# The query projection of the expert layer from unsplit weights: full fp32 products, seven chunks loaded ahead, three rows of the second table fetched early

## The chip, the cores and the metric

One core of one Trainium2 chip runs the whole program in one launch. The metric is the device time of that launch in microseconds, measured several times; beside it stands one profiled execution, whose trace gives every time in this document that is not called the median. PE is TensorE, DVE VectorE, ACT ScalarE, POOL GpSimd and SP the engine whose queue issues most weight loads.

## What is computed

256 tokens of width 2048 pass through two blocks. The first has a gated recurrence, a dilated attention and a convolutional feed-forward. The second has a recurrent and a spatial gating half and then the layer that this change touches (`peer`): 8 query heads of 256 columns, each scored against two sets of 128 keys; the best 16 of each side give 256 pairs, and the best 16 pairs name 16 of 16384 experts. So each token needs 128 rows of each of two tables, `expert_u` and `expert_v`.

```python
q = (x @ w_q).reshape(B, S, PEER_HEADS, 2, PEER_HALF)
s = jnp.einsum('bshpk,hpnk->bshpn', q, sub_keys)
top_s, top_i = lax.top_k(s, PEER_TOPK)
...
u = jnp.take(expert_u, it, axis=0)
act = jax.nn.gelu(jnp.einsum('td,tkd->tk', xt, u)) * gt
v = jnp.take(expert_v, it, axis=0)
return jnp.einsum('tk,tkd->td', act, v)
```

A final norm with `final_norm_g` follows.

## The kernel before

All weights but the tables come as one stream of blocks (`stream_blocks`), each cut into chunks of 1 MB, each chunk into two halves called subs (`sub`, numbered 0 to 751; the last 32, 720 to 751, are the weight `peer_w_q`, called `wq` below: 8 blocks of 4 subs, one block per head). SP loads chunks into a ring of `NR = 3` buffers `raw`; ACT rounds a sub to the high part `wh` (float32r) and DVE takes the low part `wl = raw - wh`; PE forms every product in three float32r matmuls (high by high, high by low, low by high). These are lines L1158, L1159 and L1160 for `wq`. `u5` holds the transposed input, itself as a high and a low part. A chunk is loaded when the chunk three before it has been split (`s_lo`), and a block's result goes to one of two pairs of banks, which ACT (L1463) copies to `qTt`. PE then multiplies with the keys (`key_scores`, L1288), ACT keeps the scores (`keep_scores`, L1613), and DVE chooses: `top_sides`, `top_pairs`, `top_ids` (its last instruction, L2154, writes the row numbers `ids` of one head for 128 tokens) and `top_weights`. Before that, `turn_keys` transposes the keys `kyN`, which POOL has loaded during the projection before `wq` (`w_out_2`, blocks 116 to 119, of which the order below shows `u` as operand).

Row n of `peer_u` is then gathered for 128 tokens at once: one indirect DMA of 128 x 8 KB = 1.049 MB, issued by POOL (`get_u`, L2253) into one of `NU = 4` buffers `Ub`. It waits for its ids and for dot n - 4 to be done. DVE forms the dot products (`dot`, L2169); each fourth time ACT takes the gelu and DVE multiplies by the gates. Row n of `peer_v` goes likewise (`get_v`, L2261) into one of `NV = 11` buffers `Vb`, and PE adds it, times a diagonal matrix from ACT (`diag`), to the output banks (`spread`, L1303). There are 256 rows of each table. `get_v` waits until PE has taken the last sub of all (`s_taken`), since `Vb` lies where `raw`, `wh`, `wl` and `u5` were.

The order of the instructions on each engine is laid out beforehand by `Plan`: it keeps a modelled clock per engine, prices each step, and lets tasks (attention, scan, choose, begin) put their steps between the subs when their inputs are ready by that clock. Each engine then walks the same list. `begin` puts the first gathers and dots between the subs of `wq`; after the last sub ("streamed") a fixed loop alternates `get_v`, `get_u`, `dot` and `spread`.

## Time and profile before

| | us |
|---|---|
| median of 3 runs (3550.36 to 3556.91) | 3554.09 |
| the profiled execution | 3544.8 |
| its span, first to last instruction | 3542.9 |
| first sub of `wq` on PE | 2163.4 |
| first ids written, first gather | 2196.8, 2197.05 |
| last key scores on PE | 2269.7 |
| first gather of `peer_v` issued | 2272.3 |

The profiled execution has 1.9 us around its span, and is 9.3 us shorter than the median. Its span falls into a part up to about 2197 us, in which PE is the busy engine, and a part of 1346 us in which gathers run. Granted clock over the span: 0.981.

### The profile page before, as it was taken

The page shows a single profiled execution, that of the slowest core. Times are in us where ns is not written, and L with a number is a line of the kernel's source. Part 1 is how long each engine was busy: PE and PEld are TensorE (multiplying, and loading weights), DVE is VectorE, ACT ScalarE, POOL GpSimd, SP SyncE. Part 2 cuts the span into 40 slices and gives each one's busy share as a digit, 9 for nine tenths or more (in the row PEclk, how much of TensorE's full clock was granted, in tenths as well). Part 3 has the DMA queues.
Part 4 walks back from the last instruction along what each step waited for, and adds up shares of the span by engine and source line. Part 5 has one row for each costly group of instructions (what it writes and reads, how often), then busy time and mean ns, then how long its engine had stood idle before and what let it go on. Part 6 is the DMA issues. An engine that isn't in the chain of part 4 may idle for free.

```text
span 3542.9 us, 35558 instructions
## 1 busy us (share of the span) xinstructions
PE 3147.4 (89%) x13774; PEld 2290.1 (65%) x13774; DVE 2276.9 (64%) x3508; ACT 1287.5 (36%) x1890; POOL 531.3 (15%) x533
## 2 busy tenths in 40 slices
PE   7999999999999999999999889887777777777776
PEld 6998988888877888888887779733232323222222
DVE  7776767775556777775566667777677644444444
ACT  5555555554435555554346644311111111000001
POOL 0000000000000000000000000444333433333332
PEclk9999999999999999999999999999999999999999
DMA  6545555556555555556564456899999999999998
GB/s 212 167 140 157 161 169 165 171 167 202 185 174 163 188 183 183 184 190 214 190 210 153 143 174 210 324 420 420 420 420 420 420 420 420 420 420 420 420 420 338
DMA packets 405744, 936.97 MB, mean 264 GB/s; under 512 B 16487, under 2 KB 246536, under 8 KB 339144
## 3 DMA queue, kind: packets, MB, share of 16 engines
q0 software_dynamic: 75936, 547.39, 37.5%
q1 hardware_dynamic: 328624, 386.96, 34.1%
q8 instruction: 109, 1.79, 0.2%
q10 hardware_dynamic: 1016, 0.35, 0.0%
q14 instruction: 59, 0.48, 0.0%
HBM read 932.54 MB, written 2.10 MB: 264 GB/s over the span
## 4 chain that ended last, share of the span: by engine, by line
PE 58%; DMA 31%; DVE 7%; ACT 2%; issue 1%; POOL 1%; POOLq 0%; ACTq 0%; SPq 0%; DVEq 0%
DMA Ub<-in_peer_u,ids 29%; PE W L1155 13%; PE W L1163 11%; PE W L1165 10%; PE W L1164 10%; PE W L1153 7%; DVE Ub L2169 4%; PE M L1215 1%; PE W L1152 1%; DMA Vb<-in_peer_v,ids 1%; POOL Vb L2261 1%; ACT wh L1381 0%; DMA raw<-in_peer_w_q 0%; DVE wl L1759 0%; PE W L1158 0%
## 5 line engine op out<-in xcount | busy, mean ns | idle before, releaser
L1759 DVE TENSOR_TENSOR wl<-raw,wh 128x1024 fp32r<-128x1024 f32 (+1 forms) x752 | 881.6, 1188 | 630.4 <-ACT wh L1381 628.5
L1381 ACT ACTIVATE wh<-raw 128x1024 fp32r<-128x1024 f32 (+1 forms) x752 | 763.1, 1030 | 843.9 <-PE W L1165 613.6
L2169 DVE CUSTOM_DVE_ANT_0 Ub<-Ub,xn 128x2048 f32<-128x2048 f32 x256 | 586.3, 2291 | 483.5 <-DMA Ub<-in_peer_u,ids 483.4
L1155 PE MATMUL W<-u,wh 128*128 128x512 f32 x2040 | 723.3, 398 | 0.0
L1303 PE MATMUL W<-Vb,diag 128*128 128x512 f32 x1008 | 466.6, 607 | 164.1 <-DMA Vb<-in_peer_v,ids 108.4
L1153 PE MATMUL W<-u,wl 128*128 128x256 f32 x2176 | 602.9, 282 | 0.2 <-DVE u L1721 0.2
L1163 PE MATMUL W<-wh,u 128*128 128x512 f32 (+1 forms) x1280 | 491.3, 384 | 6.8 <-DVE wl L1759 4.9
L1165 PE MATMUL W<-wh,u 128*128 128x512 f32 (+1 forms) x1280 | 480.2, 375 | 0.0
L1164 PE MATMUL W<-wl,u 128*128 128x512 f32 (+1 forms) x1280 | 480.0, 375 | 0.0
L1303 PEld LDWEIGHTS W<-Vb,diag 128*128 128x128 f32 x1008 | 183.3, 191 | 447.3 <-issue 365.9
L1155 PEld LDWEIGHTS W<-u,wh 128*128 128x128 f32 x2040 | 384.1, 188 | 89.2
L1153 PEld LDWEIGHTS W<-u,wl 128*128 128x128 f32 x2176 | 412.5, 190 | 6.1 <-issue 0.5
L1303 PE MATMUL M<-Vb,diag 128*128 128x512 f32 x512 | 268.7, 650 | 143.1 <-ACT diag L1635 76.6
L1628 ACT ACTIVATE dots<-dots 128x4 f32<-128x4 f32 x64 | 13.1, 205 | 1045.0 <-DVE dots L2169 1045.0
L2253 POOL DMA_INDIRECT Ub<-in_peer_u,ids x256 | 251.6, 983 | 821.1 <-DVE dots L2169 707.9
L1303 PEld LDWEIGHTS M<-Vb,diag 128*128 128x128 f32 x512 | 94.7, 200 | 301.5 <-issue 193.2
L2261 POOL DMA_INDIRECT Vb<-in_peer_v,ids x256 | 269.0, 1051 | 78.5 <-issue 75.8
L1163 PEld LDWEIGHTS W<-wh,u 128*128 128x128 f32 x1280 | 242.5, 189 | 42.1 <-DVE wl L1759 5.7
L1165 PEld LDWEIGHTS W<-wh,u 128*128 128x128 f32 x1280 | 242.0, 189 | 36.3
L1164 PEld LDWEIGHTS W<-wl,u 128*128 128x128 f32 x1280 | 242.7, 190 | 34.5
L1303 PE MATMUL T<-Vb,diag 128*128 128x512 f32 x512 | 245.4, 602 | 0.0
L1303 PEld LDWEIGHTS T<-Vb,diag 128*128 128x128 f32 x512 | 101.2, 198 | 131.4 <-issue 131.4
(333 smaller groups left out, 3192.4 us busy)
## 6 DMA issues: line engine op xcount, KB each, us to landing
raw<-in_w_in SPq DMA_DIRECT2D x128, 1024.0 KB, 5.3
raw<-in_w_up SPq DMA_DIRECT2D x88, 1024.0 KB, 5.3
raw<-in_w_down SPq DMA_DIRECT2D x44, 1024.0 KB, 5.2
raw<-in_w_in SPq DMA_DIRECT2D x144, 256.0 KB, 3.7
raw<-in_w_out SPq DMA_DIRECT2D x32, 1024.0 KB, 5.2
raw<-in_w_proj_a SPq DMA_DIRECT2D x16, 1024.0 KB, 5.1
raw<-in_peer_w_q SPq DMA_DIRECT2D x16, 1024.0 KB, 5.8
raw<-in_w_proj_b SPq DMA_DIRECT2D x4, 1024.0 KB, 5.1
```

Of the source, the lines that this page charges most:

```text
L1152: q.matmul(o, vh, u[:, :, kk, :], start=True, stop=False)
L1153: i = q.matmul(pr[h][:, 0:T], vl, xh, start=False, stop=False)
L1155: i = q.matmul(o, vh, u[:, :, kk, :], start=False, stop=last)
L1163: q.matmul(o, th, H[:, k, :], start=first, stop=False)
L1164: q.matmul(o, th, L[:, k, :], start=False, stop=False)
L1165: i = q.matmul(o, tl, H[:, k, :], start=False, stop=last)
L1303: i = q.matmul(out_banks[t][j][:, :], diag[:, n % 4, :], Vb[n % NV][:, CK[j]], start=k == 0, stop=k == 127 or n + 1 in ASIDE)
L1381: q.activation(wh[:, s % NS, 0:b.half], r, ACT.Copy).then_inc(s_hi, 1)
L1759: q.tensor_tensor(wl[:, s % NS, 0:b.half], r, wh[:, s % NS, 0:b.half].bitcast(F32), SUB).then_inc(s_lo, 1)
L2169: q.tensor_tensor_reduce(U[:, :], U[:, :], xn[:, t, :], 1.0, 0.0, MUL, ADD, dots[t][:, k:k + 1]).then_inc(s_dot, 1)
L2253: q.indirect_dma_start(Ub[n % NU][:, :], None, eu, bass.IndirectOffsetOnAxis(ids[t][:, k:k + 1], 0)).then_inc(s_u[n % NU], 16)
L2261: q.indirect_dma_start(Vb[n % NV][:, :], None, ev, bass.IndirectOffsetOnAxis(ids[t][:, k:k + 1], 0)).then_inc(s_v[n % NV], 16)
```

## The change

`wq` is no longer split. SP loads its 16 chunks into `Wb`, seven buffers of 8 KB per partition that lie over `raw`, `wh` and `wl`. Chunks 0 to 2 go where `raw` was, on the same condition as before; chunks 3 to 6 wait until PE has taken the last split sub (`s_taken >= split_subs`); a later one waits until PE is through with the chunk seven before it. PE forms each product with one fp32 matmul (`whole`) from `Wb` and an unsplit `u5`, so `u5` takes half its former room, and ACT and DVE each turn one half of it. The converts of the last 32 subs are gone from ACT and DVE.

In the freed room there are 12 buffers for `peer_v`. The first three of them (two before `Wb`, one over `g2`) are free before `wq` is through, and `EARLY = 3` gathers of `peer_v` are issued right behind the first four of `peer_u`; they wait only for `xn`. The final gain is loaded to `gf`, over the turned keys, after the last key scores.

In the plan a split tall sub of role `both` costs 0.35 per product pair instead of 0.347, an unsplit one 0.431; `turn_keys` may start 20 us after its block instead of 6; and dots wait for the weights of their head.

```diff
-NV = 11
+NV = 12
+NW = 7
+EARLY = 3
...
-            self.taken[s] = self.put("PE", b.kc // 2 * 2 * (0.347 if b.both else 3 * (0.0134 + b.n / 2400)), t, "sub", s)
+            self.taken[s] = self.put("PE", b.kc // 2 * 2 * (0.35 if b.both else 0.431 if b.whole else 3 * (0.0134 + b.n / 2400)), t, "sub", s)
...
     def turn_keys(self):
-        t = self.clock["PE"] + 6.0
+        t = self.clock["PE"] + 20.0
...
         for n in range(NU):
             self.gather(n, t)
+        for m in range(EARLY):
+            self.add("get_v", m)
+            self.put("DMA", 2.6, t)
         for n in range(upto):
-            t = yield "DVE", lambda: self.when(("u", n), "xn")
+            t = yield "DVE", lambda: self.when(("u", n), "xn", ("chosen", 0, n // 16))
...
+                if b.whole:
+                    i = c - plan.split_subs // 2
+                    if i < NR:
+                        e.wait_ge(s_lo, 2 * (c - NR) + 2)
+                    elif i < NW:
+                        e.wait_ge(s_taken, plan.split_subs)
+                    else:
+                        e.wait_ge(s_taken, 2 * (c - NW) + 2)
+                    q.dma_start(Wb[slot_of[i % NW]][:, :].rearrange("p (k n) -> p k n", n=b.n), source(c)).then_inc(s_whole[i % NW], 16)
+                    continue
...
+            def whole(s, b, k0, n):
+                i = s // 2 - plan.split_subs // 2
+                w = Wb[slot_of[i % NW]][:, s % 2 * b.half:(s % 2 + 1) * b.half].rearrange("p (k n) -> p k n", n=b.n)
+                e.wait_ge(s_whole[i % NW], 16 * (i // NW + 1))
+                if s == b.first:
+                    e.wait_ge(s_pair[n % 2], plan.pair[n])
+                for k in range(b.kc // 2):
+                    kk = k0 + k
+                    operand_ready(b, kk)
+                    for h in range(2):
+                        m = q.matmul(pairs[n % 2][h][:, 0:T], w[:, k, col(h)], u5[:, kk, :], start=kk == 0, stop=kk == b.kt - 1)
+                m.then_inc(s_taken, 1)
...
             def get_v(n):
                 t, k = divmod(n, 128)
-                e.wait_ge(s_taken, len(subs))
+                e.wait_ge(s_xn, 8)
+                if n >= EARLY:
+                    e.wait_ge(s_taken, len(subs))
```

On PE, in the projection before `wq`, the first transposes of the keys (`kyN`) stood right behind the first transposes of `X` in the kernel before:

```order
L1165 MATMUL W3<-wh_76,u_74 128x512
L1106 MATMUL T0<-ident_49,X_73 128x128 x4
L1106 MATMUL T1<-ident_49,X_73 128x128 x4
L1277 MATMUL M0<-ident_49,kyN_180 128x128 x4
L1163 MATMUL W2<-wh_76,u_74 128x512
L1164 MATMUL W2<-wl_77,u_74 128x512
```

In the changed kernel they stand 60 rows, five subs, further on:

```order
L1223 MATMUL W3<-wl_77,u_74 128x512
L1224 MATMUL W3<-wh_76,u_74 128x512
L1336 MATMUL M0<-ident_49,kyN_181 128x128 x4
L1222 MATMUL W2<-wh_76,u_74 128x512
L1223 MATMUL W2<-wl_77,u_74 128x512
```

On DVE, where the first head is chosen, converts (`wl`) stood between the steps, here between `top_sides` (ending in `cand`), `top_pairs` (ending in `pos`) and `top_ids`:

```order
L2130 TENSOR_TENSOR cand_154<-tsv_156 128x256
L1759 TENSOR_TENSOR wl_77<-raw_75,wh_76 128x1024 x2
L2113 MAX bs_159<-cand_154 128x8
L2115 MAX_INDEX pos_160<-bs_159,cand_154 128x8
L2117 MATCH_REPLACE cand_154<-bs_159,cand_154 128x256
L2119 MAX bs_159<-cand_154 128x8
L2121 MAX_INDEX pos_160<-bs_159,cand_154 128x8
L1759 TENSOR_TENSOR wl_77<-raw_75,wh_76 128x1024
L2141 TENSOR_SCALAR pi_161<-pos_160 128x16
```

Now they follow each other:

```order
L2195 TENSOR_TENSOR cand_154<-tsv_156 128x256
L2178 MAX bs_159<-cand_154 128x8
L2180 MAX_INDEX pos_160<-bs_159,cand_154 128x8
L2182 MATCH_REPLACE cand_154<-bs_159,cand_154 128x256
L2184 MAX bs_159<-cand_154 128x8
L2186 MAX_INDEX pos_160<-bs_159,cand_154 128x8
L2206 TENSOR_SCALAR pi_161<-pos_160 128x16
```

On POOL, which issues the gathers in this order and waits at each, 14 gathers of `peer_u` stood ahead of the first of `peer_v`; these are its last two and what followed:

```order
L2253 DMA Ub0_174<-in_peer_u_2,ids0_166 128x2048
L2253 DMA Ub1_175<-in_peer_u_2,ids0_166 128x2048
L2261 DMA Vb0_181<-in_peer_v_2,ids0_166 128x2048
L2261 DMA Vb1_182<-in_peer_v_2,ids0_166 128x2048
L2261 DMA Vb2_183<-in_peer_v_2,ids0_166 128x2048
```

Now three of `peer_v` (the third into `Vg`) stand behind the first four of `peer_u`, and then 28 of `peer_u` follow (up to row 31; `...` stands for 26 of them) before row 3 of `peer_v`:

```order
L2318 DMA Ub3_178<-in_peer_u_2,ids0_166 128x2048
L2328 DMA Vb0_182<-in_peer_v_2,ids0_166 128x2048
L2328 DMA Vb1_183<-in_peer_v_2,ids0_166 128x2048
L2328 DMA Vg_184<-in_peer_v_2,ids0_166 128x2048
L2318 DMA Ub0_175<-in_peer_u_2,ids0_166 128x2048
...
L2318 DMA Ub3_178<-in_peer_u_2,ids0_166 128x2048
L2328 DMA Vb3_192<-in_peer_v_2,ids0_166 128x2048
L2328 DMA Vb4_193<-in_peer_v_2,ids0_166 128x2048
```

In the first block the order also moves in many places by a step or two, where attention and scan are laid between the subs.

## Rows read from the trace of the kernel before

**Rows 1.** The page: span, and the chain that ended last by engine.

```profile
span 3542.9 us, 35558 instructions
...
PE 58%; DMA 31%; DVE 7%; ACT 2%; issue 1%; POOL 1%; POOLq 0%; ACTq 0%; SPq 0%; DVEq 0%
```

**Rows 2.** Stretches: us, busy (x) of each engine, granted clock, DMA share, GB/s.

```profile
2163.40:2197.00 33.60, 33.60 (x283) 33.56 (x282) 30.70 (x70) 18.15 (x27) 0.00 (x0) 1.00 0.54 171
2197.00:2272.30 75.30, 68.74 (x560) 68.14 (x558) 53.47 (x70) 29.73 (x49) 22.86 (x14) 0.97 0.81 291
2272.30:3523.00 1250.70, 945.00 (x2015) 376.03 (x2016) 723.63 (x1157) 142.70 (x390) 497.74 (x498) 0.97 1.01 420
3523.00:3543.00 20.00, 7.82 (x19) 3.17 (x17) 10.70 (x14) 4.52 (x11) 0.00 (x0) 0.80 0.18 70
```

**Rows 3.** Timeline of PE: start, us, instruction, idle before and releaser.

```profile
2098.41 1.11 PE L1277 MATMUL M<-ident,kyN 128*128 128x128 f32 x4 [5.87 <-DMA kyN<-in_peer_sub_keys]
2103.00 0.60 PE L1277 MATMUL M<-ident,kyN 128*128 128x128 f32 x4
...
2163.37 0.28 PE L1158 MATMUL W<-u,wh 128*128 128x256 f32 x1
...
2169.12 1.04 PE L1106 MATMUL M<-ident,X 128*128 128x128 f32 x8
...
2178.72 1.05 PE L1288 MATMUL M<-kyT,qTt 128*128 128x128 f32 x8
...
2269.68 1.16 PE L1288 MATMUL M<-kyT,qTt 128*128 128x128 f32 x8 [0.75 <-ACT qTt L1463]
```

**Rows 4.** Timeline of PE: two fp32 products of 256 columns, one after another.

```profile
1932.98 0.59 PE L1261 MATMUL M<-xc,lw 128*128 128x256 f32 x2
1933.41 0.59 PE L1262 MATMUL M<-xc,lw 128*128 128x256 f32 x2
```

**Rows 5.** Timelines of DVE and ACT: from the first scores to the first ids.

```profile
2182.92 0.29 DVE L2113 MAX8 tsv<-sc 128x8 f32<-128x128 f32 x1
...
2187.03 2.35 DVE L1759 TENSOR_TENSOR wl<-raw,wh 128x1024 fp32r<-128x1024 f32 x2
...
2191.68 1.21 DVE L1759 TENSOR_TENSOR wl<-raw,wh 128x1024 fp32r<-128x1024 f32 x1
...
2196.59 0.18 DVE L2154 CAST ids<-sel 128x16 uint32<-128x16 f32 x1
```

```profile
2179.94 0.82 ACT L1613 ACTIVATE sc<-M,rstd 128x256 f32<-128x256 f32 x2
```

**Rows 6.** DMA queues from 2197 to 2272.3 us: packets, MB, share of 16 engines.

```profile
q1 hardware_dynamic: 7632, 8.59, 34.2%
```

**Rows 7.** Timelines of POOL, DVE and PE: gathers issued, one dot, two rows spread.

```profile
2261.38 2.74 POOL L2253 DMA_INDIRECT Ub<-in_peer_u,ids  x1 [7.38 <-DVE dots L2169]
...
2267.07 1.91 POOL L2253 DMA_INDIRECT Ub<-in_peer_u,ids  x1 [0.30 <-issue]
...
2272.31 0.94 POOL L2261 DMA_INDIRECT Vb<-in_peer_v,ids  x1 [0.30 <-issue]
```

```profile
2258.81 2.29 DVE L2169 CUSTOM_DVE_ANT_0 Ub<-Ub,xn 128x2048 f32<-128x2048 f32 x1
```

```profile
2289.89 1.88 PE L1303 MATMUL M<-Vb,diag 128*128 128x512 f32 x4
...
2293.33 1.88 PE L1303 MATMUL M<-Vb,diag 128*128 128x512 f32 x4
```

**Rows 8.** Line L2253 from 2245 to 2272 us: issue in ns (min/median/max), landing.

```profile
L2253 POOL DMA_INDIRECT Ub<-in_peer_u,ids x6: 1678/2122/2742, 2249.0 to 2269.3; - x6
...
DMA to landing us min/median/max: 6.3/7.3/8.1
```

**Rows 9.** Stretches of the first block, columns as in the second group.

```profile
0.00:100.00 100.00, 78.16 (x385) 66.18 (x386) 69.82 (x142) 53.70 (x72) 3.17 (x11) 0.97 0.64 209
...
0.00:960.00 960.00, 929.90 (x5015) 824.85 (x5016) 663.09 (x1226) 499.91 (x695) 4.23 (x13) 0.99 0.55 172
```

More of the change, by code:

```diff
@@ L208, in __init__ @@
             b.end = len(self.subs)
+        self.split_subs = min(b.first for b in self.blocks if b.whole)
         self.parts = [sum(3 if self.chunks[i][0].n == 384 else 1 for i in range(c % NR, c + 1, NR))
@@ L303, in convert_upto @@
     def convert_upto(self, end):
-        while self.next_conv < min(end, len(self.subs)):
+        while self.next_conv < min(end, self.split_subs):
             s = self.next_conv
@@ L312, in convert_upto, with loaded @@
             self.next_conv += 1
+    def loaded(self, s):
+        c = s // 2
+        if c not in self.landed:
+            i = c - self.split_subs // 2
+            free = self.taken[s - 2 * NW + 1] if i >= NW else self.taken[self.split_subs - 1] - 8.0
+            self.landed[c] = max(free + 5.0, self.landed[c - 1] + 4.0)
+        return self.landed[c]
     def operand(self, b):
@@ L332, in stream @@
                 self.until(lambda: self.when(*turned))
-            t = max([self.lo[s] + 0.1] + [self.ready.get(x, 0.0) for x in turned])
+            t = max([self.loaded(s) if b.whole else self.lo[s] + 0.1] + [self.ready.get(x, 0.0) for x in turned])
             if s == b.first:
@@ L469, in turn_block @@
             t2 = self.put("PE", 0.9, t2, "turn", ep, k)
-            bank.free = self.put("DVE", 0.9, self.put("ACT", 0.9, t2))
+            if ep == 5:
+                bank.free = self.put("DVE", 0.45, self.put("ACT", 0.45, t2))
+            else:
+                bank.free = self.put("DVE", 0.9, self.put("ACT", 0.9, t2))
             self.done(("turned", f"u{ep}", k // 2), bank.free)
@@ L934, in program @@
         kyN = at("kyN", [16, P], Z + 16384)
-        area = Area(u0 + 32768, Z)
-        Vb = [area.get(f"Vb{i}", [D]) for i in range(7)]
-        area = Area(END - 32768, END)
-        Vb += [area.get(f"Vb{i}", [D]) for i in range(7, NV)]
+        Vb = [area.get(f"Vb{i}", [D]) for i in range(EARLY - 1)]
+        Vb.append(at("Vg", [D], g2_at))
+        area = Area(raw0, Z)
+        Wb = [area.get(f"Wb{i}", [2048]) for i in range(NW)]
+        area = Area(raw0, Z)
+        Vb += [area.get(f"Vb{i}", [D]) for i in range(EARLY, EARLY + 7)]
+        area = Area(END - 16384, END)
+        Vb += [area.get(f"Vb{i}", [D]) for i in range(EARLY + 7, NV)]
         banks = {n: ctx.enter_context(nc.psum_tensor(n, [P, 512], F32))
@@ L945, in program @@
         s_raw = [sem(f"raw{i}") for i in range(NR)]
+        s_whole = [sem(f"whole{i}") for i in range(NW)]
         s_hi, s_lo, s_taken = sem("hi"), sem("lo"), sem("taken")
@@ L1000, in program @@
         CK = [slice(512 * j, 512 * (j + 1)) for j in range(4)]
+        slot_of = [(plan.split_subs // 2 + i) % NR for i in range(NR)] + list(range(NR, NW))
         def col(k):
@@ L1359, in turn @@
                     v = banks[name][:, :].rearrange("p (k t) -> p k t", k=2)
-                    q.activation(uh[ep][:, k:k + 2, :], v, ACT.Copy).then_inc(s_bank[name], 1)
+                    q.activation(uh[:, k:k + 2, :], v, ACT.Copy).then_inc(s_bank[name], 1)
                     return
@@ L1363, in turn @@
                 e.wait_ge(s_kept, 1 if gain is cst1 else 3)
-                q.activation(uh[ep][:, k, :], banks[name][:, 0:T], ACT.Copy, scale=gain[:, g0 + k:g0 + k + 1])
-                q.activation(uh[ep][:, k + 1, :], banks[name][:, T:2 * T], ACT.Copy,
+                if ep == 5:
+                    q.activation(u5[:, k, :], banks[name][:, 0:T], ACT.Copy, scale=gain[:, g0 + k:g0 + k + 1]).then_inc(s_bank[name], 1)
+                    return
+                q.activation(uh[:, k, :], banks[name][:, 0:T], ACT.Copy, scale=gain[:, g0 + k:g0 + k + 1])
+                q.activation(uh[:, k + 1, :], banks[name][:, T:2 * T], ACT.Copy,
                              scale=gain[:, g0 + k + 1:g0 + k + 2]).then_inc(s_bank[name], 1)
```

41 lines of the change are left out of this document (26 added, 15 removed).

## The prediction, made before the changed kernel ran

> **What bounds the kernel now.** I read the chain that ended last first: PE carries 58% of it and DMA 31% [rows 1]. The share of DMA has to lie in one piece to be a bound, so I asked for stretches next [rows 2]. They show the border. Up to 2197 us PE is busy all the time (33.60 of 33.60 us) and the DMA engines half (0.54). From 2272.3 to 3523 the DMA engines are full (1.01, 420 GB/s), whatever the others do. A gather of 128 x 8 KB is 1.049 MB, so 2.50 us at that rate; 512 of them are 1279 us. In between, from 2197 to 2272.3, the share is 0.81: 19% of 75.3 us, 14.3 us, is DMA time that nobody used although ids were there. After 3523 there are 20 us of finish, which the change doesn't touch.
>
> So everything behind the first ids is a sum of DMA time. The end lies at: time of the first ids + 512 gathers + what else the DMA engines move after that time + the gaps between transfers + 20 us. A step of PE, ACT or DVE counts only if it moves one of these terms. For the kernel before: the ids are written at 2196.8 [rows 5]. The hardware queue moved 8.59 MB up to 2272.3 [rows 6]; less 1.05 for the final gain that is 7.2 chunks of `wq`. It held 34.2% of 75.3 us, 25.8 us for 8.2 units of 1.05 MB, so 3.1 us a chunk. Sum: 2196.8 + 1279 + 7.2 x 3.1 (22.3) + final gain and first half of the output 5 + gaps 14.3 = 3517, against 3523 in the trace. The 6 us that are missing I carry over unchanged.
>
> **Change 1: the keys are turned later.** PE stood still for 5.87 us, since `kyN` had not landed, and the four transposes behind the wait took 1.11 us where the next four took 0.60 [rows 3]. PE is the busy engine of this stage, so both are on the path. Five subs later (12 matmuls of 512 columns each, some 2.9 us a sub, worked out from 48 matmuls of half that width in 5.75 us [rows 3]) the keys are there. What is next late at the old place: nothing that the trace shows, for the sub behind it had its operands. **-6.4 us**, and everything behind moves with it. In the next steps I leave this shift out and add it at the end.
>
> **Change 2: the first ids.** Old product: 48 matmuls from 2163.37 to 2169.12 [rows 3], 0.12 us each, 0.36 a product. New product: L1261 starts 0.43 before L1262 [rows 4], one fp32 product of 256 columns in two records; that is this very shape. The first key scores stand behind 40 products in both kernels, plus 0.8 for transposes. Before: 2163.4 to 2178.7, 15.3 us. Now 40 x 0.43 + 0.8 = 18.0, so 2181.4, 2.7 later. Before, ACT kept the scores from 2179.94 to 2180.8, but DVE only began at 2182.92 [rows 5]: it was behind with converts and `xn`. Now ACT is through at 2183.4 and DVE, without converts, is free. From there the choice took 13.9 us with three converts of together 3.4 us inside it (2.35 + 1.21, less overlap) [rows 5]; now 10.5. Ids at 2194.0 instead of 2196.8: **-2.8 us**. Upper bound of this saving: the price of PE's 2.7 was nothing and DVE could start at once, 5.5; lower: DVE starts as late after ACT as it did (2.1), 0.7.
>
> The Trainium skill, FP8 and Floating Point Precision, TensorE Precision Notes, says that a true fp32 product takes four passes through the array. By that, and 0.12 us for a pass, a product would be 0.48 and the ids would come at 2196.0, a gain smaller by 2 us. The trace, with 0.43, shows less.
>
> **Change 3: fewer chunks behind the ids.** Chunks 0 to 2 are loaded as before. Chunks 3 to 6 go out at once when PE has taken the last split sub, 2163.4; four chunks are 12.4 us of a queue that was half empty (0.54). A chunk holds PE for 16 x 0.43 = 6.9 us, so by 2194 four more are released, the last just then. Ten have landed and 6 are left, instead of 7.2: 1.2 x 3.1 = **-3.8 us** (between 0 and 7). No chunk is late: number i is wanted at 2164 + 6.9 i and asked for 48 us before that.
>
> **Change 4: the gaps behind the ids.** PE's `wq` now takes 256 x 0.43 = 110 us instead of 92, and it is the last sub that opens `get_v` from row 3 on: at 2163.4 + 110 + 0.8 + 8 key scores of 0.8 = 2281, where the last key scores were at 2269.7 [rows 3]. This is hidden if gathers of `peer_u` fill the time. POOL has 32 of them and 3 of `peer_v` ahead of that wait; with 6 chunks they are 35 x 2.5 + 18.6 = 106 us, from 2194 to past 2300. So the queue ahead of `get_v` ends 19 us after PE: that is the cover. (ACT's gelus of these dots stand ahead of its copies of `qTt`, so PE will wait for dots and end late too; it costs nothing while the DMA engines are full.) Behind 2300 the free buffers of `peer_v` are asked for at once, 1.2 us each. Then rows 3 to 27 of `peer_v` flow without any of `peer_u`, and here PE is the slower one: a row's spread takes 3.44 us (2289.89 to 2293.33 [rows 7]) against 2.50 for its gather. Row 12 + k needs the buffer of row k. If the spreads begin 4 us after the first of these gathers (last key scores, keeping them), row 12 + k is asked for 4 + 3.44 (k + 1) us after it and wanted after 2.5 (9 + k) less 2: that holds up to k = 13 or 14, row 26. So about 1 us is lost, and each further us that the spreads start later is lost too, until the gathers of `peer_u` come back at row 32.
>
> What decides is whether four buffers `Ub` keep the DMA engines full by themselves, after the chunks have run out at about 2230. One buffer's round: 0.3 us from the dot (2258.81 to 2261.1) to POOL (2261.38) [rows 7], 7.3 from issue to landing [rows 8], 2.3 for the dot [rows 7]: 9.9, a fourth of it 2.47, just the 2.50 of the transfer. Lower end: landing in 6.3, 2.2 a row, gap nothing. Upper end: POOL's issues at 2261.38 and 2267.07 are two apart, 2.85 a row [rows 7], a gap of 0.35 for each of 27 rows, 9.5 us. I take 2.6, near the round's own sum: 27 x 0.1 = 3 us. To it come the 1 us of `peer_v`, 2 us until the first transfer flows, and 3 while DVE chooses the second head (10.5 us without a dot, while 7 gathers and a chunk or two are under way). Gaps 9 instead of 14.3: **-5.3 us**, with ends at -12 (only the first 2 us left) and +1 (9.5 + 6).
>
> In rows of the profile POOL's issue takes 0.94 us when DVE has no dot [rows 7] and 1.68 to 2.74 beside dots [rows 8]; its landing time of 7.3 has that in it. The Trainium skill, GPSIMD Engine Reference, Key points, says that POOL shares its SBUF interfaces with DVE and contends with DVE instructions that read two SBUF inputs, which a dot does. The trace agrees with its 2.74. It speaks against this change, which puts 29 dots where 11 were.
>
> **The rest** is priced at nothing. Converts leave ACT and DVE, which PE didn't wait for here. The halves of `u5` are shorter. The twelfth `Vb` adds depth to a full queue. The final gain stays one unit behind the ids. `top_ids` of the heads 2 to 5 now run while only `peer_v` flows, 44 us of DVE within 25 gathers of 2.5.
>
> **Sum:** -6.4 - 2.8 - 3.8 - 5.3 = **-18.3**. Span 3542.9 - 18 = 3525, execution 3527; the median, 9.3 above the profiled one before, 3554 - 18 = **3536**.
>
> **The rivals.**
> - *The ring of four is the bound* (contention of dots and issues, 2.85 to 3.0 us a row): gaps of 15.5 to 19.5, so a gain of 12 to 8. For it: the spacing of the issues. Against it: those issues stood behind a backlog of dots, which a DMA-bound ring doesn't have. Time 3544.
> - *The new order in the first block.* PE is idle for 30.1 us up to 960, 21.8 of them in the first 100 [rows 9], so 8.3 can be saved there at most, and a new stall of the same kind costs as much. I find no place where it must appear. It shifts any case by some 4 us either way.
> - *The change does little*: the bytes are the same, the gaps of before come back in other places (second head, start of `peer_v`) and chunks still compete; only the keys count, 6.4 less. Time 3548, about no change.
> - *Slower.* `get_v` opens late and the ring leaves DMA idle. Without `peer_v` each row beyond 2.5 us is lost 27 times; the other gains are 13 us and the gaps of before 14.3, of which 6 are used: at (13 + 8.3) / 27 = 0.79 above 2.5, at 3.3 us a row, the gain is gone. At 3.6 (landing in 11.8 instead of 7.3) it is 8 us slower: 3562. Nothing in the rows is that slow with one queue at work.
> - *More than forecast*: no gaps but the start, the ids at their upper bound, and a stall less in the first block: -28 and beyond, 3526 or less.
>
> **How the numbers follow.** Within 0.2% is within 7 us of 3554, which is about what can be told from no change here. Forecast (gain 14 to 27) 0.55; ring bound (7 to 14) 0.20; more than 27 0.08; little 0.10; slower 0.07. The second rival widens each. Range 3521 to 3549: down to a gain of 33 (sum of the lower ends, 6.4 + 5.5 + 7 + 12 = 31, and a little of the first block), up to 5, which leaves out the slower case and a part of the one with little effect, 0.13 in all. Faster 0.83, same 0.11, slower 0.06.
>
> **What would show it.** No wait for `kyN` on PE. Fp32 products 0.43 us apart. First ids near 2188 (2194.0 - 6.4). Up to 2300 a DMA share above 0.9, gathers of `peer_u` 2.5 to 2.6 apart after the last chunk, row 3 of `peer_v` issued near 2295. From there 420 GB/s, but for a us or two near its row 26, up to about 3505. The prediction is wrong if the share between the chunks' end and that issue stays near 0.8, if PE waits for a chunk or for its bank pair before the first ids, or if the first sub of `wq` is not 6 us earlier than now.

## The result, and the profile after

The changed kernel took 3516.04 us (median of 4 executions, 3514.08 to 3523.43) beside 3555.43 for the one before (four too, 3550.36 to 3556.91). The ratio of their means is 0.9896, its 95% interval 0.9878 to 0.9913; all ratios below are of means. The profiled execution took 3514.93, its span is 3513.1: 29.8 us less than before, where 18.3 were forecast. 3516 lies 20 below the forecast of 3536, and below its range of 3521 to 3549.

The page, as in [rows 1]:

```profile
span 3513.1 us, 34930 instructions
...
PE 61%; DMA 28%; DVE 7%; POOL 2%; ACT 2%; issue 1%; POOLq 0%; ACTq 0%; SPq 0%; DVEq 0%
```

The stretches, cut where those of [rows 2] were (first product of `wq`, first ids, row 3 of `peer_v` issued, 20 us before the end):

```profile
2154.00:2184.90 30.90, 30.90 (x152) 27.36 (x151) 19.82 (x59) 5.26 (x10) 0.00 (x0) 1.00 0.75 239
2184.90:2289.40 104.50, 93.51 (x434) 81.32 (x433) 78.92 (x115) 16.04 (x44) 55.93 (x35) 0.94 1.01 399
2289.40:3493.00 1203.60, 926.54 (x2014) 370.09 (x2015) 676.07 (x1092) 133.86 (x374) 479.26 (x477) 0.99 1.01 418
3493.00:3513.00 20.00, 7.95 (x19) 3.23 (x17) 10.70 (x14) 4.52 (x11) 0.00 (x0) 0.82 0.23 89
```

The line to read is the second: 1.01 from the ids on, where the kernel before had 0.81. Cut finer, the same trace shows 1.02 to 1.06 from 2190 to 2260, with chunks on their way, and 0.92 from 2270 to 2280, when they are through (three packets of their queue in these 10 us): about 1 us. The one larger hole behind the ids is where gathers of `peer_u` come back after those of `peer_v`; this is POOL's wait there, and the stretch around it:

```profile
2361.38 0.94 POOL L2328 DMA_INDIRECT Vb<-in_peer_v,ids  x1 [0.30 <-issue]
2372.51 0.94 POOL L2318 DMA_INDIRECT Ub<-in_peer_u,ids  x1 [10.19 <-DVE dots L2234]
```

```profile
2360.00:2400.00 40.00, 40.00 (x94) 17.67 (x93) 27.05 (x57) 7.48 (x17) 19.87 (x15) 1.00 0.93 360
```

0.93 instead of 1.01 in 40 us is 3 us. Next PE, against [rows 3]: the keys (first and last of their transposes), first product of `wq`, first and last key scores.

```profile
2104.05 0.60 PE L1336 MATMUL M<-ident,kyN 128*128 128x128 f32 x4
...
2117.28 0.60 PE L1336 MATMUL M<-ident,kyN 128*128 128x128 f32 x4
...
2154.02 3.61 PE L1184 MATMUL W<-u,Wb 128*128 128x256 f32 x16
...
2172.16 1.05 PE L1347 MATMUL M<-kyT,qTt 128*128 128x128 f32 x8
...
2286.51 1.57 PE L1347 MATMUL M<-kyT,qTt 128*128 128x128 f32 x8 [2.40 <-ACT qTt L1525]
```

The wait of 5.87 us is gone. Sixteen records, eight products, take 3.45 us from the first to the instruction behind them (2154.02 to 2157.47): 0.43 a product. The choice of the first head on DVE, against [rows 5], first step and last:

```profile
2174.12 0.29 DVE L2178 MAX8 tsv<-sc 128x8 f32<-128x128 f32 x1 [8.29 <-ACT sc L1675]
...
2184.72 0.17 DVE L2219 CAST ids<-sel 128x16 uint32<-128x16 f32 x1
```

DVE is waiting for the scores, and the choice takes 10.8 us without a convert in it. Last POOL (against [rows 7, 8]): issues ahead of row 3 of `peer_v`, and their landing.

```profile
2268.25 2.80 POOL L2318 DMA_INDIRECT Ub<-in_peer_u,ids  x1 [1.78 <-DVE dots L2234]
...
2286.77 2.34 POOL L2318 DMA_INDIRECT Ub<-in_peer_u,ids  x1 [0.30 <-issue]
2289.42 0.94 POOL L2328 DMA_INDIRECT Vb<-in_peer_v,ids  x1 [0.30 <-issue]
```

```profile
L2318 POOL DMA_INDIRECT Ub<-in_peer_u,ids x8: 2182/2308/2803, 2268.3 to 2286.8; - x8
...
DMA to landing us min/median/max: 6.8/6.9/7.0
```

Eight rows in 21.2 us are 2.65 a row.

Where the 29.8 us of span came from, in the two traces: 1.9 before the second block's weights (the first chunk of `w_up` goes out at 1058.7 instead of 1060.6); 7.45 from there to the first product of `wq` (2163.4 to 2154.0, less 1.9); 2.5 from that to the ids (33.4 to 30.9); 17.9 behind the ids (1346.1 to 1328.2). The last is the surprise: 9.1 was forecast. The queue of the chunks moved 9.42 MB behind the ids; less 1.05 for the final gain and 2.1 for the output that is 6 chunks, as forecast, instead of 7.2, worth 3.7. So 14 us are left for gaps and for what my sum didn't explain, where 5.3 were forecast.

### The profile page after: what moved, and what is told of

It reads as the page before. It is cut to its first block, busy times and chain, and to the rows that moved or that the text cites. A ratio compares the mean times of both kernels' runs of the same rounds, so it can differ in the third digit from the quotient of the medians.

```text
span 3513.1 us, 34930 instructions
## 1 busy us (share of the span) xinstructions
PE 3151.0 (90%) x13518; PEld 2292.2 (65%) x13518; DVE 2237.5 (64%) x3468; ACT 1249.3 (36%) x1846; POOL 545.9 (16%) x533
## 4 chain that ended last, share of the span: by engine, by line
PE 61%; DMA 28%; DVE 7%; POOL 2%; ACT 2%; issue 1%; POOLq 0%; ACTq 0%; SPq 0%; DVEq 0%
DMA Ub<-in_peer_u,ids 27%; PE W L1214 13%; PE W L1222 11%; PE W L1224 11%; PE W L1223 11%; PE W L1212 7%; DVE Ub L2234 4%; PE M L1274 1%; PE M L1362 1%; PE T L1362 1%; POOL Ub L2318 1%; PE W L1211 1%; DMA Vb<-in_peer_v,ids 1%; PE W L1184 0%; POOL Vb L2328 0%
## 5 line engine op out<-in xcount | busy, mean ns | idle before, releaser
L1824 DVE TENSOR_TENSOR wl<-raw,wh 128x1024 fp32r<-128x1024 f32 (+1 forms) x720 | 842.1, 1186 | 595.7 <-ACT wh L1443 593.7
L1443 ACT ACTIVATE wh<-raw 128x1024 fp32r<-128x1024 f32 (+1 forms) x720 | 729.0, 1028 | 789.5 <-PE W L1224 595.5
L1362 PE MATMUL W<-Vb,diag 128*128 128x512 f32 x928 | 431.6, 609 | 149.9 <-DMA Vb<-in_peer_v,ids 95.9
L1362 PEld LDWEIGHTS W<-Vb,diag 128*128 128x128 f32 x928 | 169.6, 192 | 411.8 <-issue 332.0
L2318 POOL DMA_INDIRECT Ub<-in_peer_u,ids x256 | 271.5, 1060 | 748.8 <-DVE dots L2234 640.9
L1362 PE MATMUL M<-Vb,diag 128*128 128x512 f32 x468 | 230.0, 614 | 104.1 <-DMA Vb<-in_peer_v,ids 63.1
L2328 POOL DMA_INDIRECT Vb<-in_peer_v,ids x234 | 241.9, 1034 | 98.8 <-issue 67.2
L1362 PEld LDWEIGHTS M<-Vb,diag 128*128 128x128 f32 x468 | 83.3, 191 | 243.0 <-issue 178.2
L1362 PE MATMUL T<-Vb,diag 128*128 128x512 f32 x468 | 220.4, 593 | 0.0
L1362 PEld LDWEIGHTS T<-Vb,diag 128*128 128x128 f32 x468 | 89.4, 191 | 113.1 <-issue 113.1
```

Source lines behind the costliest of these rows:

```text
L1362: i = q.matmul(out_banks[t][j][:, :], diag[:, n % 4, :], Vb[n % NV][:, CK[j]], start=k == 0, stop=k == 127 or n + 1 in ASIDE)
L1443: q.activation(wh[:, s % NS, 0:b.half], r, ACT.Copy).then_inc(s_hi, 1)
L1824: q.tensor_tensor(wl[:, s % NS, 0:b.half], r, wh[:, s % NS, 0:b.half].bitcast(F32), SUB).then_inc(s_lo, 1)
L2318: q.indirect_dma_start(Ub[n % NU][:, :], None, eu, bass.IndirectOffsetOnAxis(ids[t][:, k:k + 1], 0)).then_inc(s_u[n % NU], 16)
L2328: q.indirect_dma_start(Vb[n % NV][:, :], None, ev, bass.IndirectOffsetOnAxis(ids[t][:, k:k + 1], 0)).then_inc(s_v[n % NV], 16)
```

## The experiments

Each kernel ran beside the kernel before, in four groups; its medians there were 3553.95, 3549.62, 3551.71 and 3551.18. "Rest" is the time from the first ids to the end: 1346.1 before, 1328.2 with the change.

**The two kernels again.** `before_again`, without an edit:

> The kernel before, once more. The prediction carried the 9.3 us between its profiled execution (3544.8) and its median (3554) over to the changed kernel, whose profiled execution is only 1 us under its median. Theory A: the first profile was a lucky execution; a second one lies near 3554, and the 9 us are lost between the first ids and the first gather of peer_v (gaps of more than 14 us), where chunks and gathers compete. Rival: they are spread over the whole span (clock, PE) or over the 1200 us of full DMA, and the share between 2197 and 2272 is again 0.81. Second rival: the profiled execution is again near 3545 and profiling itself makes this kernel faster.

3552.05 (3546.22 to 3557.03), ratio 0.9999 (0.9989 to 1.0009). Its profiled execution took 3546.99, and again is at the low end of its own kernel, with a share of 0.80 in the 75.3 us behind the ids. So theory A fell, and the rival's share came true. That profiling itself makes a kernel faster isn't shown either, for in `keys_only`, `keys_early` and `ring5` the profiled execution lies within 0.5 us of the median. `after_again`, likewise without an edit:

> The changed kernel once more, for its spread beside ahead8 on one chip. Theory A (executions differ only by where the granted clock dips between 1700 and 2110 us): median 3514 to 3519, and in the profiled execution the rest behind the ids 1327.5 to 1329.5 whatever its start of w_q. Theory B (executions also differ behind the ids): rest outside that range.

3517.9 (3515.78 to 3520.81), ratio 0.9908 (0.9891 to 0.9924); start of `wq` 2155.7, ids 2186.6, rest 1330.0. The median is theory A's; the rest is outside its range by half a us, and so theory B's: behind the ids too, two executions differ by some 2 us. Below, 2 us of one profile are no finding. The changed kernel's 8 executions together have the median 3517.2.

**The keys alone**, in the kernel before:

```diff
-        t = self.clock["PE"] + 6.0
+        t = self.clock["PE"] + 20.0
```

> The kernel before with one number of the change: turn_keys may start 20 us after its block instead of 6. Theory A: no wait for kyN, first sub of wq 7.4 us earlier, first ids 7.4 us earlier, and all of it in the end: 7.4 us less than before, ratio 0.9979. Rival: part of it is lost in larger gaps behind the ids; ratio 0.999 to 1.

3538.09 (3537.32 to 3547.08), ratio 0.9965 (0.9952 to 0.9979). Span 3535.8, that is 7.1 and 9.3 less than the two profiled executions of before; the medians differ by 15.9. The rest is 1346.8, unchanged: in the traces the keys move everything behind them and no more. Why the median moved by about twice as much is not shown. The length of the stall is part of it: PE waited 5.9 us for `kyN` in `before` and 6.7 in `before_again`. The opposite edit in the changed kernel, `keys_early` (20.0 back to 6.0):

> The changed kernel with the keys transposed 6 us after the planner's clock and not 20. Theory A (the wait for kyN costs its own length and nothing more): a wait of 5 to 7 us of TensorE for kyN comes back, first product of w_q 6 to 8 us later, the rest behind the ids as with the change, median 3522 to 3525. Theory B (a stall there also makes executions run at a lower granted clock, as the twice larger move of the median by the earlier run with the keys alone suggests): the profiled execution 6 to 9 us longer, but the median 3528 to 3533, with granted clocks of its executions .005 below those of the changed kernel.

3530.14 (3527.82 to 3533.81), ratio 0.9941 (0.9926 to 0.9956): 12 us above `after_again` in the median and 11.6 in the span. The wait is back, in PE's timeline:

```profile
2098.50 1.12 PE L1336 MATMUL M<-ident,kyN 128*128 128x128 f32 x4 [5.62 <-DMA kyN<-in_peer_sub_keys]
```

and so is a stretch at a lower granted clock behind it; first `keys_early`, then `after_again`:

```profile
2080.00:2100.00 20.00, 14.38 (x67) 11.93 (x67) 10.30 (x12) 6.38 (x8) 1.69 (x2) 0.93 0.79 268
2100.00:2120.00 20.00, 20.00 (x87) 16.33 (x86) 6.56 (x6) 7.44 (x10) 0.00 (x0) 0.90 0.39 131
```

```profile
2080.00:2100.00 20.00, 20.00 (x94) 16.66 (x93) 12.06 (x14) 8.15 (x9) 1.69 (x2) 1.00 0.78 267
2100.00:2120.00 20.00, 20.00 (x102) 16.62 (x101) 10.83 (x13) 9.28 (x12) 0.00 (x0) 1.00 0.59 195
```

40 us at 0.07 and 0.10 less are about 3 us. The kernel before has the same behind its wait, in one execution less (`before`, the two lines) and in the other as much (`before_again`: 0.93 and 0.90):

```profile
2080.00:2100.00 20.00, 14.13 (x66) 11.77 (x65) 10.74 (x14) 7.20 (x10) 1.69 (x2) 0.95 0.79 271
2100.00:2120.00 20.00, 20.00 (x92) 16.42 (x92) 7.83 (x8) 7.98 (x10) 0.00 (x0) 0.97 0.41 140
```

That is 1.6 us in `before`. In `keys_early` the first product of `wq` is 9.0 later (2164.7 against 2155.7): 5.6 of wait, some 3 of clock; and the rest is 2.6 longer, of which no cause was looked for. Theory A's time is too short, and theory B's median is met; but its reading, that whole executions run at a lower clock, fell: their granted clocks (.984 to .986) are those of `after_again` (.985 to .986), and the profiled execution lies at the median. What the profile shows of a stall's price beyond its length is in the stretch around and behind it.

**The first block.** `price_old`, the changed kernel with 0.35 put back to 0.347:

> The changed kernel with the planner's price of a product of the joined kind put back to 0.347 us, which restores the order in the first block alone. Theory A (the new order in the first block gave the 1.9 us by which all later work starts earlier there, and nothing else): first w_up chunk issued 1.5 to 2.5 us later than with the change, span 3514 to 3516, median 3516 to 3519. Theory B (that order gives nothing, the 1.9 us are noise of executions): start as with the change within 0.5 us, median 3515 to 3517.

3518.33 (3515.99 to 3522.46), ratio 0.991 (0.9895 to 0.9925), span 3515.9; the first chunk of `w_up` goes out at 1060.99 instead of 1058.74, 2.25 later. PE's waits from 100 to 960 us have this line; the kernel before has the same wait of 3.5 us, the changed kernel doesn't:

```profile
PE M L1245 <- ACT AT L1585: 3.5, 1, 3.5
```

Theory A, in the trace. One pair of traces would not carry it, for `after_again` sent that chunk at 1055.4, 3.4 us before its twin. All sixteen traces of this document do: with the old order it went out between 1060.3 and 1061.7 (four), with the new one between 1055.4 and 1058.9 (twelve), 3.6 us apart in the median, as much as the stall. The 1.9 us of the two profiles are near the low end of this. The medians of the times (3518.3 and 3517.2) don't tell it.

**How deep the chunks are loaded ahead.** `ahead3` and `ahead5` set NW to 3 and 5:

```diff
-NW = 7
+NW = 3
```

> The changed kernel with NW = 3: fp32 products from raw chunks, but only three chunks are loaded ahead. Theory A (the gaps went because DVE no longer has converts behind starved chunks): PE waits for chunks that the gathers starve, but DVE and the gathers go on, so the DMA engines stay full; only more chunks lie behind the ids (8 or 9 instead of 6, 3.1 us each): 6 to 10 us more than the changed kernel, ratio 1.002 to 1.003. Rival B (the depth of seven took the gaps away): 15 us or more above the changed kernel, share behind the ids back near 0.8.

> The changed kernel with five chunks of w_q loaded ahead in place of seven. Theory A (the depth matters by bytes: each chunk that is not in before the ids costs about 3.1 us of gather time, and no wait of TensorE reaches the gathers): 8 chunks behind the ids, rest behind the ids 1334 to 1336, share of the transfers 1.0 still, median 3522 to 3526. Theory B (with fewer than seven, starved chunks also hold up the choice of the first head, as with three): first ids 2 us or more later than 2185 and the rest over 1337, median 3528 or more.

`ahead3`: 3538.24 (3532.34 to 3543.45), ratio 0.9966 (0.9953 to 0.9979), 9.97 chunks behind the ids, rest 1342.5. `ahead5`: 3534.61 (3530.87 to 3538.18), ratio 0.9954 (0.9938 to 0.997), 7.97 chunks, rest 1344.1. The two are alike, and 14 to 16 us of rest above seven. By bytes `ahead3` would be 12.4 above and `ahead5` 6.2. In `ahead3` the DMA engines stayed full until 2300 (1.02 to 1.04), as its theory A has it, but with a chunk more behind the ids than it allowed, and the median came out 21 us above the changed kernel's, as rival B would have it. The surplus in `ahead5` is in POOL's timeline:

```profile
2294.68 0.94 POOL L2318 DMA_INDIRECT Ub<-in_peer_u,ids  x1 [0.30 <-issue]
2306.59 1.04 POOL L2328 DMA_INDIRECT Vb<-in_peer_v,ids  x1 [10.97 <-PE W L1184]
```

and in its stretch from 2290 to 2310, with PE's waits from 2165 to 2310:

```profile
2290.00:2310.00 20.00, 17.83 (x81) 15.13 (x81) 15.70 (x46) 3.31 (x10) 7.55 (x6) 0.92 0.67 248
```

```profile
PE W L1184 <- DMA Wb<-in_peer_w_q: 14.2, 2, 8.3
```

PE waits for a chunk, so its last product comes at 2305.9; row 3 of `peer_v` may not be issued before that; POOL stands 11 us, and the DMA engines run dry (0.67 for 20 us is 6.8 us). So theory B is right that it isn't bytes alone, and wrong in the place: the ids moved no more than the start of `wq` did. `ahead3` has 6.1 us of that wait, which left 2 us empty (0.91 from 2300 to 2320), beside its 12.4 of bytes. `ahead8` gives the room of one early row to an eighth chunk:

```diff
-NW = 7
-EARLY = 3
+NW = 8
+EARLY = 2
...
+        w7_at = area.o
+        Wb7 = area.get("Wb7", [2048])
...
+        Vb.append(at(f"Vb{EARLY + 7}", [D], w7_at))
```

> The changed kernel with eight chunks of w_q loaded ahead: the eighth lies in the room of one of the three early rows of the second table, which then has two early ones. Theory A (each chunk is worth its 3.1 us of gather time as long as TensorE does not hold up row 3 of the second table): 5 chunks behind the ids, rest behind the ids 1325 to 1327, less by up to 2 us of hole for the early row that is gone, median 3512 to 3516. Theory B (the depth has a knee between five and seven, and beyond it a chunk is worth nothing since starved chunks fill holes that come back): rest 1328 to 1331, median 3516 to 3520.

3520.02 (3511.91 to 3521.56), ratio 0.9906 (0.9888 to 0.9924), 4.97 chunks, rest 1327.8: 0.4 and 2.2 below the changed kernel's two. The rest lies between the theories, the median at the top of theory B's, and it is no better version.

**PE's work, halved.** `half_late` leaves out every second product in blocks 2 to 7 of `wq`, `half_first` in block 0 (condition `b.role[1] < 1`), so their output is another:

```diff
+                    if b.role[1] >= 2 and kk % 2 and kk != b.kt - 1:
+                        continue
```

> The changed kernel, but in blocks 2 to 7 of wq half of the products are left out (every second k), so PE has 96 products less, 41 us; the result is another. First ids unchanged. Theory A (behind the first ids only DMA time counts): the same time as the changed kernel within 2 us, although PE is through 41 us earlier; POOL still has 32 gathers of peer_u ahead of row 3 of peer_v. Rival (the 18 us that fp32 products cost PE show in the end, or peer_v opens too late): 5 to 18 us less.

> The changed kernel, but in block 0 of wq half of the products are left out (every second k), 16 products of 0.43 us, 6.9 us of PE ahead of the first key scores; the result is another. Theory A (end = first ids + DMA time behind them): first ids 6.9 us earlier, all of it in the end; as a little less of the chunks has landed by then, 5 to 7 us less than the changed kernel. Rival (the end hangs on the later part of wq or on the steady stage): no change.

`half_late`: 3518.31 (3512.99 to 3519.06), ratio 0.9905 (0.989 to 0.9919), rest 1327.6: no gain. So the work of PE's products there isn't what counts. The run doesn't show what an earlier end of `wq` would give: PE's last product still came at 2281.5 (2283.7 with the change), since PE waits 33.6 us for `qTt` behind gelus of dots and 6.9 for a chunk. `half_first`: 3515.94 (3514.18 to 3524.71), ratio 0.9904 (0.9889 to 0.9919). In its trace the ids come 25.7 us after the first product of `wq` instead of 30.9, so 5.2 of the expected 6.9 us; but that product came at 2161.1, 7 us late, and the medians don't differ. The rest is 1330.6, like that of `after_again`, which fits theory A; for the end of the kernel the run decides nothing. What of the late start the trace shows is told in the last section.

**The early rows, and the converts.** `no_early` takes away the three early gathers of `peer_v`:

```diff
-        for m in range(EARLY):
-            self.add("get_v", m)
-            self.put("DMA", 2.6, t)
...
-            if EARLY <= m < 256:
+            if 0 <= m < 256:
...
-                if n >= EARLY:
-                    e.wait_ge(s_taken, len(subs))
+                e.wait_ge(s_taken, len(subs))
```

`converts_back` is that, and ACT and DVE convert each half chunk of `wq` again (into rooms of the missing rows, which nothing reads), with PE waiting for it as before; its products stay fp32 ones. Its plan then lays fewer dots between the subs (POOL issues 22 gathers of `peer_u`, not 32, before the first row of `peer_v`), so it puts back the converts together with the order that they bring:

```diff
-                e.wait_ge(s_whole[i % NW], 16 * (i // NW + 1))
+                e.wait_ge(s_lo, s + 1)
...
+                    q.activation(Vb[0][:, half * b.half:(half + 1) * b.half], Wb[slot_of[i % NW]][:, half * b.half:(half + 1) * b.half], ACT.Copy).then_inc(s_hi, 1)
...
+                    q.tensor_tensor(Vb[1][:, g], Wb[slot_of[i % NW]][:, g], Vb[0][:, g], SUB).then_inc(s_lo, 1)
```

> The changed kernel without the three early gathers of peer_v: same 12 buffers, but all rows of peer_v wait until PE has taken the last sub. Theory A: the three rows (7.5 us of DMA) are what the DMA engines have while DVE chooses the second head; without them a gap opens there, 3 to 8 us more. Rival: the starved chunks fill that gap anyway (the share was 1.02 to 1.04 there, with five chunks waiting up to 46 us): no change.

> As no_early, but ACT and DVE again do two passes over every sub of wq (copy and difference, into the still free buffers 0 and 1 of peer_v, results not used) on the old conditions, no more than four subs ahead of PE, and PE waits for them; products, chunks and buffers as in the changed kernel. The plan then puts 19 dots instead of 29 between the subs. Theory A (the gaps of before were DVE standing behind converts that PE paces and that starved chunks hold up): the gaps come back, share between the ids and peer_v near 0.85, 10 to 18 us more than no_early. Rival (the gaps were the ring of four or the three-deep chunks): within 4 us of no_early.

`no_early`: 3524.08 (3519.84 to 3528.68), ratio 0.9925 (0.9912 to 0.9938), rest 1333.9, 5.7 more than with the change: theory A's size, but not its place. While DVE chose the second head the share was full without the early rows too (1.03 from 2200 to 2240, with chunks on their way), as the rival has it; a gap of some 2 us came only from 2240 to 2260, and where the other 3.7 lie was not found. `converts_back`: 3536.62 (3533.36 to 3538.35), ratio 0.9957 (0.9944 to 0.997), 12.5 more than `no_early`. Its ids are at 2198.2 instead of 2184.5, 13.7 later, 2.9 of which lie ahead of `wq`. And the gaps are back; first `converts_back`, then `no_early`:

```profile
2240.00:2260.00 20.00, 20.00 (x98) 17.71 (x97) 18.59 (x30) 7.72 (x11) 4.55 (x4) 1.00 0.73 286
2260.00:2280.00 20.00, 17.77 (x89) 15.35 (x87) 17.08 (x22) 6.21 (x15) 10.54 (x6) 1.00 0.61 216
```

```profile
2240.00:2260.00 20.00, 19.11 (x93) 16.60 (x92) 16.97 (x22) 3.62 (x7) 13.98 (x7) 1.00 0.91 324
2260.00:2280.00 20.00, 16.79 (x82) 14.55 (x80) 17.69 (x19) 2.53 (x8) 17.58 (x8) 1.00 0.99 389
```

That is (0.18 + 0.38) x 20 = 11 us of empty DMA, with the same ring, the same depth and the same products. The rest grew only 1.5 us over `no_early`: later ids leave fewer chunks behind them (4.86 instead of 5.97, 3.4 us less), and the stretch from 2350 to 2400 has a share of 1.01 instead of 0.93 (4 us); 2 us more I can't account for. So the end pays for the converts mainly by the ids that they delay. In the kernel before, the chain was this, by its waits from 2197 to 2272 (POOL, ACT, DVE):

```profile
POOL Ub L2253 <- DVE dots L2169: 50.3, 7, 17.3
```

```profile
ACT wh L1381 <- PE W L1160: 22.5, 14, 2.7
ACT wh L1381 <- DMA raw<-in_peer_w_q: 7.4, 1, 7.4
```

```profile
DVE wl L1759 <- ACT wh L1381: 19.7, 11, 7.2
```

Read from below: DVE stands at a convert since ACT has not made `wh`; ACT stands since PE has not freed a buffer, once since a chunk had not landed; the dots stand behind that convert in DVE's order; and POOL waits up to 17.3 us for a dot, with no buffer free.

**The ring of `peer_u`.** `ring5` (NU 5, and NV 11 and EARLY 2, so that it fits) and `ring3` (NU 3), whose edit this is:

```diff
-NU = 4
+NU = 3
```

> The changed kernel with five buffers for peer_u, eleven for peer_v and two early rows instead of 4, 12 and 3. The trace of the changed kernel has a last hole of 3 us from 2366 to 2400, where the gathers of peer_u start again and POOL waits for dots. Theory A: a fifth buffer closes some of it: 1 to 3 us less. Rival (ring of four is a bound in the steady stage): more than 5 us less. Second rival: the row of peer_v that is missing early costs as much: no change.

> The changed kernel with a ring of three buffers for rows of the first table in place of four. Theory A (the ring bounds only the stretch in which gathers of the first table stand alone, from the first ids to row 3 of the second): rows there 3.3 to 3.6 us apart after the 20th, the transfers' share in 2245 to 2290 down to .80 to .90, rest behind the ids 5 to 12 us longer than 1328, median 3520 to 3528. Theory B (four is far more than is needed, since starved chunks fill every hole): no change, median 3515 to 3518. Theory C (the ring also paces the mixed stretch): rest 25 us or more longer, median over 3540.

`ring5`: 3522.37 (3520.81 to 3525.1), ratio 0.9918 (0.9905 to 0.9931), rest 1331.6, 5 us more in the median, which no theory had. The fifth buffer closed the hole from 2350 to 2400 (1.01), but PE waits 16.2 us for chunks there, whose longest landing was 63.1 us, and POOL 18.0 for PE, with a share of 0.62 from 2280 to 2300. So this run doesn't tell what a fifth buffer alone is worth:

```profile
POOL Vb L2328 <- PE W L1184: 18.0, 1, 18.0
```

`ring3`: 3538.68 (3532.76 to 3542.49), ratio 0.9959 (0.9946 to 0.9973), rest 1351.5, 21 to 23 us more than the changed kernel's two. Part of it is where the ring stands alone, as theory A has it (two stretches of three), the rest where `peer_u` comes back after `peer_v`:

```profile
2240.00:2260.00 20.00, 20.00 (x98) 17.70 (x98) 14.73 (x16) 1.94 (x7) 8.66 (x6) 1.00 0.88 333
...
2280.00:2300.00 20.00, 17.59 (x67) 11.77 (x66) 10.79 (x12) 4.29 (x10) 10.26 (x8) 1.00 0.80 308
...
2350.00:2400.00 50.00, 50.00 (x118) 22.22 (x117) 28.62 (x76) 10.79 (x24) 19.13 (x16) 1.00 0.74 272
```

0.13, 0.21 and 0.27 short of 1.01: 2.6, 4 and 13.5 us, where four buffers leave 3 us from 2350 to 2400 and 1 before (0.97 from 2260 to 2280). From 2400 on the share is 1.01 with three as with four, so theory C's pacing of the mixed stretch is wrong beyond that place. Four is nearly enough, and the price of one less is steep.

## Why the prediction was wrong

Its account of the bound was right: the end is the ids, plus bytes, plus gaps. The direction and the four changes that it named came true; the sum was short. The rival "more than forecast", given 0.08, had the direction of the miss, but with no more than 12 us from gaps.

- *Keys, 6.4.* Measured 7.45 between the two profiles, 7.1 to 9.3 by `keys_only`, 9.0 by `keys_early`. I took the wait and the slower transposes right behind it (0.5 us), and left out that the granted clock is lower over the whole 40 us around and behind the wait: 1.6 us in the profile of before, 3.4 in `keys_early`. In medians the keys were worth more than the start of `wq` shows, 12.2 us (`keys_early`) and 15.9 (`keys_only`); the cause of the surplus stays open.
- *First ids, 2.8.* Measured 2.5. The product took 0.43, as in the row of fp32 products. The 0.48 of my other estimate was four times the 0.12 us of a split product. Whether there are four passes, as the Trainium skill says (FP8 and Floating Point Precision, TensorE Precision Notes), no run here shows; what the trace refutes is my 0.12 us for one.
- *Chunks, 3.8.* 7.2 to 6 behind the ids, as counted. But "no chunk is late" was luck of a size that I hadn't seen. I took the landing of a chunk from a stage without gathers (`raw<-in_w_in` 5.3 us). Behind the ids the five chunks landed after a median of 32.3 us and at most 46.4; "asked for 48 us before" was just enough. With five ahead it wasn't, and PE's waits for chunks, 14.2 us, became 7 us of empty DMA.
- *Gaps, 5.3: the step that failed.* I priced the new gaps one by one, 9 us in all, and each of them as if nothing else was there to send. Measured: 4 us, 1 at 2270 to 2280 and 3 from 2360 to 2400. The start and the choice of the second head are holes in the stream of gathers, and they came to about nothing, for the chunks that were waiting flowed into them: from 2220 to 2230 the gathers' queue held 60.8% of the DMA engines' time and the chunks' 44.5%. That reading rests on the traces, where the chunks' packets and the full share stand side by side; no run here removes the chunks from the holes. The ring's 0.1 us a row was hidden only as long as there were chunks, and cost the 1 us behind them. What the runs do show is part of the cause of the old gaps. By what the sum leaves over (next point), they and the remainder were 19.8 us before, 16.3 in `converts_back`, 11.4 in `no_early` and 5.7 with the change: 4.9 by the converts with the order they bring, 5.7 by the three early rows, each uncertain by some 2 us. The converts emptied 11 us between 2240 and 2280, but gave a part back further on. The first 3.5, which came with chunks loaded seven deep and with the room for them, no run separates. I had named DVE "free" in the step on the ids, and not drawn from it what the old gaps would lose.
- *The 6 us "missing" in my sum*, carried over unchanged, shrank with the gaps. Rest before: 1279 + 22.3 + 5 + 20 is 1326.3 of 1346.1, so 19.8 for gaps and remainder, of which the share of 0.81 accounts for 14.3; after: 1279 + 18.5 + 5 + 20 is 1322.5 of 1328.2, so 5.7. Forecast was 15. What the remainder consists of stays open.
- *The cover of 19 us for PE.* In the trace PE's last product came at 2283.7 and row 3 of `peer_v` at 2289.42: 5.7 us. `wq` took 129.7 us, not 110, with waits for `qTt` (9.7 us), a clock of 0.94 and the key scores that stand between its blocks. Since the cover held, it cost nothing; `ahead5`, `ahead3` and `ring5` are what it looks like when it doesn't.
- *First block, 0.* One stall of 3.5 us less on PE gave 1.9 between the two profiles and 3.6 between the medians of all traces. I had this as a shift of either sign; it was inside its bound.
- *Ring of four.* 2.65 us a row against 2.6, and 1 us lost in all: the rival of 2.85 to 3.0 us a row fell. What paces the last eight rows is POOL and DVE in step. Seven of these issues waited for nothing but took 2.31 us (median), since each began beside a dot and ended 0.8 us after that dot had ended. This holds without exception for the 28 issues from 2185 to 2600 us that began beside a running dot (0.80 to 0.82), and for the 13 of the kernel before from 2197 to 2600; an issue of the changed kernel that began beside none took 0.93 to 1.17. The Trainium skill (GPSIMD Engine Reference, Key points) says that there is contention between the two; by these rows the issue isn't slowed but held until the dot is over. It costs about 0.1 us a row over the transfer's 2.5.
- *The offset from profile to median, 9.3.* The 29.8 us of span would give 3524 by it. The changed kernel's 8 executions lie 2.3 us above its profiled one, those of `before_again` 5.1. A single profiled execution of before lay at the low end of a spread of 12 us (3544.8 to 3556.9), and I carried that as if it belonged to the program. With the keys alone the offset was already down to 0.5 us, so a part of what I call offset here may be the keys' doing, which no run here settles. This is 8 of the 20 us by which 3536 was off; the span's 11.5 are first block 1.9, keys 1.0 and gaps 8.9, less 0.3 by the ids.

## What to carry to other kernels

When DMA is the bound, ask of each hole in its stream who stood ahead of the instruction that would have freed a buffer: here converts that waited for PE, in the same queue as dots that waited for nobody. A second stream that may wait (weights loaded seven deep) costs its bytes and fills holes, as long as it is asked for early enough: here a chunk feeds PE for 6.9 us, so seven deep is 48 us ahead, and beside the gathers the longest landing was 46.4. Five deep was short of that and cost 16 us of rest, of which 6.2 were bytes, since a late chunk holds up all that its consumer opens. And take a kernel's time from several executions, not from the profiled one and an offset.

## What was unexpected of the hardware

- **The same idle time, another clock.** `half_first` and the changed kernel have the same work up to `wq`, and PE was busy for the same 16.98 us of the stretch from 1880 to 1900. The granted clock was 0.83 in one and 1.00 in the other, and again differed from 2050 to 2080. First the changed kernel, then `half_first`:

```profile
1880.00:1900.00 20.00, 16.98 (x77) 13.82 (x75) 10.56 (x14) 10.27 (x15) 0.00 (x0) 1.00 0.47 158
...
2050.00:2080.00 30.00, 22.16 (x101) 18.35 (x100) 22.70 (x29) 12.00 (x14) 0.00 (x0) 0.89 0.41 139
```

```profile
1880.00:1900.00 20.00, 16.98 (x63) 13.49 (x62) 9.63 (x14) 9.61 (x14) 0.00 (x0) 0.83 0.44 147
...
2050.00:2080.00 30.00, 22.16 (x95) 18.27 (x94) 23.13 (x29) 10.92 (x13) 0.00 (x0) 0.77 0.34 116
```

  By such stretches, and by the 3.4 us that executions already differ at 1058 us, the start of `wq` lay between 2152.7 (`half_late`) and 2161.1 us (`half_first`) in kernels with the same code ahead of it. Whether PE's pause of 3 us there costs clock or not is open in each execution: what decides it no run here shows. The Trainium skill (TensorE: Matmul & The Clock Gate, Part 1) says that the unit which watches PE runs free of the kernel's start; that would allow such differences between executions, and the two rows agree with it, but no run here tests it.
- **A chunk among gathers lands late.** A load of 1 MB of `w_in` landed after 5.3 us (median), the seven of `wq` that were issued before 2160 us after 7.2 (median), and after 32.3 us (median of five, longest 46.4) behind the first ids, while gathers of `peer_u` landed in 9.6. A chunk's time includes its wait behind earlier chunks of the same queue, of which up to three were still out. These are packets, MB and share by queue in the changed kernel from 2184.9 to 2225, gathers (q0) and chunks (q1):

```profile
q0 software_dynamic: 1665, 12.20, 74.3%
q1 hardware_dynamic: 3660, 3.70, 27.9%
```

  Gathers go in pieces of 7.3 KB and chunks in pieces of 1.0 KB, and two pieces of a chunk pass for one of a gather. The Trainium skill (DMA: Bandwidth & Descriptors, Queues, rings and completion order) says that a DMA engine goes round the queues that have work and takes a whole packet, of several descriptors, from each. Whether the pieces counted here are such packets, no row shows. If they were, and went one for one, the chunks would get an eighth of the bytes; the trace gives them 3.70 of 15.9 MB, nearly twice that.
- **The full share moves less there.** 399 GB/s with chunks among the gathers, 418 to 420 without, at the same share of 1.01: a chunk's 1.05 MB hold the DMA engines 3.1 us, a gather's 2.5.
